# Transposed modulation tiles, two up projections ahead of their norm's root, and first weight blocks split in halves by three engines

## The chip, the cores and the metric

One core of one Trainium2 chip runs the kernel. The metric is the device time of one execution in microseconds. It was 2487.04 us in the median of three runs of the kernel before (2485.96 to 2487.86). Engines are named as in the profile: PE (TensorE), PEld (its weight loads), DVE (VectorE), ACT (ScalarE), POOL (GpSimd), SP (SyncE, which here only issues transfers).

## The reference

512 tokens of 1024 features pass two hybrid layers and a diffusion-style block with neighbourhood attention; everything is float32.

```python
def hybrid_layer(x, ...):                       # twice
    cb, cc, cu, q, k, v, g, ga, gb = split(rmsnorm(x, norm_mix) @ w_in)
    merged = sigmoid(ga) * short_conv_mixer(cb, cc, cu) + sigmoid(gb) * retention_mixer(q, k, v, g)
    x = x + merged @ w_o
    return x + square(relu(rmsnorm(x, norm_mlp) @ w_up)) @ w_down
# once, after rmsnorm(x, norm_final); h and hc are the modulated norms of x and of the context
sh1, sc1, g1, sh2, sc2, g2 = split(silu(c) @ w_mod + b_mod)      # also for c_ctx: csh1, csc1
q, k, v = heads(h @ w_q), heads(h @ w_k), heads(h @ w_v)         # 16 heads, kc and vc from hc
x = x + g1 * (neighbourhood_attention(q, k, v, kc, vc, rpb) @ w_o)
h2 = rms_norm(x, norm2) * (1 + sc2) + sh2
a, g = split(h2 @ ffn_w_up)                                      # 2816 features each
x = x + g2 * ((a * gelu(dwconv3(g))) @ ffn_w_down)
```

## The kernel before, in words

The stream X stays in SBUF, features on the partitions (8 tiles of 128), tokens along the columns (512). Every dense product is made to float32 accuracy from three products of reduced parts: high x high, high x low, low x high (`product`, L526). Weights arrive in blocks of 128 output features (128x1024, 512 KB) in a ring of four slots. SP issues the transfers; ACT copies a block to its high part (L987; the first three in `first_high`, L1054); POOL subtracts to get the low part in four operations of 256 columns (`low`, L464); PE then runs the block's job of 24 products into PSUM bank n % 4, and DVE or ACT evacuates it. Semaphores count: `w_hi_ready`, `w_lo_ready` (blocks), `jobs_done` (jobs), `bank_free` (evacuated), `tiles_ready` (input tiles split).

**Start.** SP issues X and the first four blocks alternately; ACT issues parameters (L976) and positions (L977) and waits for both. It then makes for each pair of X tiles the high parts H_hi (L1027), one block's high part, and squares (L1078). DVE makes H_lo (L1330), the rope angles and the sum of squares. The value job comes first; unlike the others it takes tokens as stationary operand, and a block holds two k tiles of 512 value columns, so one tile is 12 products. After two of the eight blocks PE sums the squares (L548, L550), ACT takes the root (L1020, L1022), DVE the reciprocal (L1367, L1368). DVE evacuates the values in two batches (L1471 to L1309), then q and k, then decays the retention scores (ST, L1309).

**Modulation.** In each of the eight groups of the two layers' feed-forward parts, ACT fetches six tiles of modulation weights (3 MB), DVE multiplies by the condition and adds over the eight k tiles (L1662; in layer 0 also four context tiles, `ctx_acc`). What is left is a sum over the partitions. PE makes it by a product of each 128x128 tile with a two-column tile of ones (L680, L685), into one PSUM bank; at a layer's end DVE adds the bias (L1701) and makes the gains.

**Attention.** For each of eight pairs of heads (t) there are four steps (p). PE turns probabilities (L793, transposes against an identity), computes the next scores (L780), weighs values (L809, L813). The order of all this, and of the dense jobs of the next heads and of the output projection's first products that fill the gaps, is written out by hand. `output(m, first, last)` is output job m's products for k tiles first to last - 1; tile k exists once the k-th pair of heads is done. `turn_values` transposes values (L763).

**Before FF2.** Output jobs 0 to 3 are opened during the attention, job 4 has its weights in a place of its own (`wo_hi`), 5 to 7 follow. DVE adds each to X (L1881) and sums squares (L1321, L1325). PE sums over partitions in two parts (`split_sum`, L839, L841), ACT takes the root (L1022), DVE the reciprocal (L1723), then `adaptive` makes the eight input tiles: scaled (L1726, DVE), high (L1066, ACT), low (L1738, DVE).

**FF2.** 22 pairs of up jobs (gate, value) in three groups, each followed by down jobs. ACT copies the gate (L1283), DVE convolves it (L1901 to L1906), ACT applies gelu (L1286), DVE multiplies by the value job's bank (L1911) and splits. In a round of four jobs ACT's loop (`phase`) alternates one block's high part (`ahead`) with its gates.

## Time and profile before

| | us |
|---|---|
| median of the runs | 2487.04 |
| profiled execution, its own time | 2488.34 |
| its span | 2486.5 |
| PE busy | 2449.0 |
| POOL busy | 1380.8 |
| DVE busy | 1291.5 |
| ACT busy | 819.5 |

The span reaches from the first to the last instruction. PE's busy time includes the overlap of pipelined products, so its pace is read from the distance between the starts of two products rather than from the length of one. A row of the timeline gives start, duration, engine, line, operation, output and inputs, the number of merged instructions, and in brackets the engine's idle time before it and what ended it.

### The profile page before, as it was taken

How to read it: one execution, taken by the hardware profiler on the slowest of the kernel's cores; microseconds unless marked ns; L12 is line 12 of the kernel's file. 1: busy time of each engine (PE TensorE's matmuls, PEld its weight loads, DVE VectorE, ACT ScalarE, POOL GpSimd, SP SyncE). 2: the span in 40 equal slices, each digit the busy share in tenths (PEclk: the TensorE clock that was granted, in tenths of full speed). 3: DMA queues.
4: the chain of work that ended last, by engine and by line, in shares of the span. 5: the costliest groups of instructions: out<-in, count | busy, mean ns of one | idle time of the engine just before them, and what ended most of it. 6: DMA issues, size and time to landing. Idle time of an engine off the chain costs nothing.

```text
span 2486.5 us, 33193 instructions
## 1 busy us (share of the span) xinstructions
PE 2449.0 (98%) x11372; PEld 2004.7 (81%) x11372; DVE 1291.5 (52%) x1828; ACT 819.5 (33%) x1053; POOL 1380.8 (56%) x1676
## 2 busy tenths in 40 slices
PE   7999999999999999999999999999999999899999
PEld 6888888888888888888888888888777776788887
DVE  8984412354645659944123535438866665533323
ACT  4232232231211222322322311114567774432222
POOL 6556655656666655566556566647332334455654
PEclk9999999999999999999999999999999999999999
DMA  5213223243334222133232433443211112232322
GB/s 177 93 60 97 97 93 101 93 146 129 114 136 144 96 96 87 60 98 96 93 101 93 147 133 109 144 152 102 67 52 39 60 47 69 77 100 93 101 93 93
DMA packets 64455, 247.46 MB, mean 100 GB/s; under 512 B 7152, under 2 KB 9584, under 8 KB 63088
## 3 DMA queue, kind: packets, MB, share of 16 engines
q1 hardware_dynamic: 61920, 217.87, 27.0%
q10 hardware_dynamic: 2448, 28.43, 2.9%
q8 instruction: 54, 0.88, 0.1%
q14 instruction: 33, 0.27, 0.0%
HBM read 244.17 MB, written 2.10 MB: 99 GB/s over the span
## 4 chain that ended last, share of the span: by engine, by line
PE 89%; DVE 7%; DVEq 2%; issue 1%; ACT 1%; DMA 0%; ACTq 0%
PE ps L526 84%; PE ps L793 1%; PE ps L780 1%; PE ps L809 1%; PE ps L748 1%; DVE A_lo L1309 1%; DVE A_lo_f L1505 1%; DVEq L1306 0%; DVEq L1503 0%; DVE V_lo L1309 0%; DVE C_hi_f L1501 0%; DVE A_hi L1307 0%; ACT prob L1195 0%; DVE C_hi_f L1500 0%; PE ps L813 0%
## 5 line engine op out<-in xcount | busy, mean ns | idle before, releaser
L464 POOL TENSOR_TENSOR w_lo<-w_raw,w_hi 128x256 fp32r<-128x256 f32 x1612 | 1334.9, 859 | 1005.9 <-ACT w_hi L987 873.6
L526 PE MATMUL ps<-H_hi,w_hi 128*128 128x512 f32 x1952 | 776.2, 398 | 6.6 <-DVE H_lo L1738 6.6
L526 PE MATMUL ps<-H_hi,w_lo 128*128 128x512 f32 x1952 | 762.3, 391 | 0.0
L526 PE MATMUL ps<-H_lo,w_hi 128*128 128x512 f32 x1952 | 762.1, 390 | 0.0
L987 ACT ACTIVATE w_hi<-w_raw 128x1024 fp32r<-128x1024 f32 x400 | 421.3, 1056 | 989.7 <-PE ps L526 955.4
L526 PEld LDWEIGHTS ps<-H_hi,w_hi 128*128 128x128 f32 x1952 | 368.0, 189 | 90.4 <-issue 16.3
L526 PEld LDWEIGHTS ps<-H_lo,w_hi 128*128 128x128 f32 x1952 | 368.2, 189 | 78.6 <-issue 4.8
L526 PEld LDWEIGHTS ps<-H_hi,w_lo 128*128 128x128 f32 x1952 | 367.7, 188 | 77.4
L526 PE MATMUL ps<-A_lo,w_hi 128*128 128x512 f32 x552 | 215.3, 390 | 0.0
L526 PE MATMUL ps<-A_hi,w_hi 128*128 128x512 f32 x496 | 193.0, 389 | 0.0
L526 PE MATMUL ps<-A_hi,w_lo 128*128 128x512 f32 x496 | 192.9, 389 | 0.0
L1342 DVE TENSOR_TENSOR X<-X,ps 128x512 f32<-128x512 f32 x80 | 55.0, 688 | 206.4 <-PE ps L526 206.1
L526 PE MATMUL ps<-C_hi,w_hi 128*128 128x512 f32 x384 | 149.4, 389 | 0.0
L526 PE MATMUL ps<-C_lo,w_hi 128*128 128x512 f32 x384 | 149.4, 389 | 0.0
L526 PE MATMUL ps<-C_hi,w_lo 128*128 128x512 f32 x384 | 149.4, 389 | 0.0
L526 PEld LDWEIGHTS ps<-A_lo,w_hi 128*128 128x128 f32 x552 | 104.1, 189 | 21.1
L1644 DVE TENSOR_TENSOR E<-ps,rstd 128x512 f32<-128x512 f32 x64 | 44.2, 690 | 128.3 <-PE ps L526 127.7
L526 PEld LDWEIGHTS ps<-A_hi,w_hi 128*128 128x128 f32 x496 | 93.1, 188 | 19.5 <-DVE A_lo L1309 0.2
L526 PEld LDWEIGHTS ps<-A_hi,w_lo 128*128 128x128 f32 x496 | 93.1, 188 | 19.4
L526 PE MATMUL ps<-B_hi,w_hi 128*128 128x512 f32 x248 | 98.3, 396 | 0.0
L526 PE MATMUL ps<-B_hi,w_lo 128*128 128x512 f32 x248 | 97.3, 392 | 0.0
L526 PEld LDWEIGHTS ps<-C_hi,w_hi 128*128 128x128 f32 x384 | 72.1, 188 | 15.0
(255 smaller groups left out, 2911.3 us busy)
## 6 DMA issues: line engine op xcount, KB each, us to landing
w_raw<-weights SPq DMA_DIRECT2D x404, 512.0 KB, 3.5
mod_w<-mod_weights ACTq DMA_DIRECT2D x8, 3072.0 KB, 10.9
X<-x SPq DMA_DIRECT2D x4, 512.0 KB, 7.5
out<-X SPq DMA_DIRECT2D x8, 256.0 KB, 2.0
toeplitz<-biases SPq DMA_DIRECT2D x14, 128.0 KB, 2.0
decay_sb<-decay ACTq DMA_DIRECT2D x1, 1024.0 KB, 5.1
ctx_sb<-context ACTq DMA_DIRECT2D x1, 1024.0 KB, 15.4
mask_sb<-key_mask ACTq DMA_DIRECT2D x1, 320.0 KB, 3.0
```

Source lines behind the costliest of these rows:

```text
L464: last = nc.gpsimd.tensor_tensor(lo[:, c:c + LOW_COLS], w_raw[:, q, c:c + LOW_COLS], hi[:, c:c + LOW_COLS].bitcast(F32), ALU.subtract)
L526: mm = nc.tensor.matmul(dst, w[l], xs[r], start=start and a == 0, stop=stop and a == 2)
L748: nc.tensor.matmul(dst, block_sb[:, :], src[:, :], start=True, stop=True).then_inc(sum_ready[kind], 1)
L780: mm = nc.tensor.matmul(ps[:, SCORE_BANKS[head], :], (q_hi, q_lo)[l][rows, T % 2, i * P:(i + 1) * P], (k_hi, k_lo)[r][rows, first:first + ...
L793: mm = nc.tensor.transpose(ps[:, TURN_BANK, c * P:(c + 1) * P], prob[:, head, at_col:at_col + P], ident_sb[:, :])
L809: nc.tensor.matmul(ps[cols[head], OUT_BANK, o0:o0 + 2 * P], v_sb[:, T % 2, tile, cols[head]], pt[:, head, c, :, :].rearrange("p t n -> p ( ...
L987: nc.scalar.activation(w_hi[:, s, :], w_raw[:, s, :], ACT.Copy).then_inc(w_hi_ready, 1)
L1309: V.tensor_tensor(lo, whole, hi.bitcast(F32), ALU.subtract).then_inc(ready, 1)
L1342: V.tensor_tensor(X[:, m, :], X[:, m, :], ps[:, q, :], ALU.add).then_inc(bank_free, 1)
L1505: V.tensor_tensor(Alf[:, m, :], Cf[:, 0, :], Cf[:, 1, :], ALU.add)
L1644: V.tensor_tensor(E[:, q % 2, :], ps[:, q, :], rstd[:, :], ALU.mult).then_inc(bank_free, 1)
```

## The change

**Modulation.** Each modulation tile is transposed on PE against the identity (10 tiles a group in layer 0, 6 in layer 1, into banks 5 to 7), and DVE sums along the columns after each group (`mod_reduced`). The identity is loaded at the start, to a place of its own, not before the attention. DVE also splits the shift SH2 in two reduced parts.

**Start.** The wait for the positions moves to DVE, ahead of the angles. Blocks 0 and 1 are made in halves: high halves by ACT between its H_hi tiles, first low half by DVE, second by POOL. Squares come one pair later; the sum over partitions stands after the third block in layer 0.

**Attention's end.** The output products are distributed otherwise over the gaps of the last two pairs of heads, `turn_values(7, 1)` is moved, job 4 gets bank 5 and is opened in the last step (`output_ahead`), job 5 gets weights of its own (`w5_hi`, `w5_lo`).

**Late root.** ACT and DVE split X times gain (without the root) into C_hi and C_lo as each output tile is added, and ACT makes the squares. The first two FF2 jobs (gate 0, value 0) run on these parts. DVE multiplies the two banks by the root afterwards; what the shift adds to each output feature comes from 32 two-column products (`up_shifts`). The first round of FF2 is taken out of the loops.

```diff
 # PE
-                        if i == 0 and q == 2:
+                        if i == 0 and q == (2 if L else 3):
                             norm_sum(2 * L, True)
-                        pe.wait_ge(w_lo_ready, n0 + i * RING + (q + 1))
+                        halves = L == 0 and i == 0 and q < 2
+                        if halves:
+                            pe.wait_ge(first_low, q + 1)
+                        else:
+                            pe.wait_ge(w_lo_ready, n0 + i * RING + (q + 1))
...
                     pe.wait_ge(mod_summed, L * FF_GROUPS + g + 1)
-                    for s in range(MOD_GROUP):
-                        at_col = (g * MOD_GROUP + s) * 2
-                        mm = nc.tensor.matmul(ps[:, MOD_BANK, at_col:at_col + 2], mod_w[:, s, 0:P],
-                                              ones[:, 0:2], start=True, stop=True)
...
+                    pe.wait_ge(mod_reduced, L * FF_GROUPS + g)
+                    summed = [mod_w[:, s, 0:P] for s in range(MOD_GROUP)]
                     if L == 0:
+                        summed += [ctx_acc[:, s, :] for s in range(MOD_CTX)]
+                    for s, src in enumerate(summed):
+                        mm = nc.tensor.transpose(ps[:, MOD_BANK + s // TOK, s % TOK * P:(s % TOK + 1) * P], src,
+                                                 ident_sb[:, :])
                     mm.then_inc(mod_used, 1)
...
+            def up_shifts(n):
+                pe.wait_ge(shift_split, 1)
+                for q in range(2):
+                    for k in range(DT):
+                        for part, w in enumerate(weight_tiles(n + q, k)):
+                            mm = nc.tensor.matmul(ps[:, SHIFT_BANK, 2 * q:2 * q + 2], w, shift_parts[:, k, :],
+                                                  start=k == 0 and part == 0, stop=k == DT - 1 and part == 1)
+                mm.then_inc(shift_mm, 1)
...
                     if t == TILES - 2 and p == 3:
-                        output(0, 5, 6)
-                        output(1, 0, 1)
+                        turn_values(T, 1)
+                        output(1, 3, 4)
                     if t == TILES - 1 and p == 0:
-                        output(1, 4, 6)
+                        output(2, 0, 2)
                     if t == TILES - 1 and p == 1:
-                        output(2, 3, 5)
-                    if t == TILES - 1 and p >= 2:
-                        output(3, 2 * p - 2, 2 * p)
+                        output(3, 0, 2)
+                    if t == TILES - 1 and p == 2:
+                        output(3, 4, 6)
+                    if t == TILES - 1 and p == 3:
+                        output_ahead(0, 2)
...
+                    if t == TILES - 1 and p == 3:
+                        output_ahead(2, 3)
...
                     if t == TILES - 2 and p == 2:
-                        output(0, 2, 5)
-                        turn_values(T, 1)
+                        output(0, 2, 6)
+                        output(1, 0, 3)
                     if t == TILES - 2 and p == 3:
-                        output(1, 1, 4)
+                        output(1, 4, 6)
                     if t == TILES - 1 and p == 0:
-                        output(2, 0, 3)
+                        output(2, 2, 6)
                     if t == TILES - 1 and p == 1:
-                        output(2, 5, 6)
-                        output(3, 0, 2)
-            for m in range(WO_AHEAD):
-                output(m, 6, 7)
+                        output(3, 2, 4)
+                    if t == TILES - 1 and p == 2:
+                        for m in range(WO_AHEAD):
+                            output(m, 6, 7)
+            output_ahead(3, 5)
             for m in range(WO_AHEAD):
                 output(m, 7, DT)
+            output_ahead(5, DT)
...
-            split_sum(2 * DEPTH + 1, last_squared, 1)
...
                 if g == 0:
                     pe.wait_ge(w_lo_ready, n + 2)
...
+                    up_shifts(n)
+                    split_sum(2 * DEPTH + 1, wo_squared, DT)
+                    pair_job(n, 0, wo_parts, 0, C_hi, C_lo)
+                    pair_job(n, 2, tiles_ready, ATT_TILE + DT, H_hi, H_lo)
 # ACT
-            act.wait_ge(par_loaded, 32)
+            act.wait_ge(par_loaded, 16)
             for j in range(X_PARTS):
...
                     stream_high(m, PAR_NORM1, 0)
-                if j < RING - 1:
+                    if j < 2:
+                        first_half(j, m % X_PART)
+                if j == 2:
                     first_high(j)
...
+            act.dma_start(ident_sb[:, :], ident).then_inc(ident_loaded, 16)
...
+                        act.wait_ge(w_loaded[1], (WO_ROUND + 2) * 16)
+                        act.wait_ge(ctx_mm, 2 * TILES)
+                        nc.scalar.activation(w5_hi[:, :], w_raw[:, 1, :], ACT.Copy).then_inc(w_hi_ready, 1)
+            def wo_parts_high(m):
+                act.wait_ge(bank_free, WO_JOB + m + RING + 1)
+                nc.scalar.activation(E[:, SQUARES[m % 2] if m else SUMSQ, :], X[:, m, :],
+                                     ACT.Square).then_inc(wo_squared, 1)
+                nc.scalar.activation(C_hi[:, m, :], X[:, m, :], ACT.Copy,
+                                     scale=gains[:, 2 * DT + m:2 * DT + m + 1]).then_inc(wo_high, 1)
+            for m in range(DT):
+                wo_parts_high(m)
+                if m < 2:
+                    ahead_at(WO_JOB + 6 + m)
+                if m >= RING:
+                    ahead_at(WO_JOB + RING + m)
             root(2 * DEPTH + 1, E[:, ROOT, :])
-            high_parts(1, SH2)
+            high_parts(1, SH2, WO_JOB + DT + RING)
...
+                if g == 0:
+                    gate(r, 0, 0)
+                    ahead(r, 2)
+                    gate(r, 0, 2)
+                    ahead(r, 3)
+                    tile0, rounds = m0 + 2, rounds - 1
 # DVE
+            def first_low_half(q):
+                dve.wait_ge(first_split, q + 1)
+                V.tensor_tensor(w_lo[:, q, 0:V_WIDE], w_raw[:, q, 0:V_WIDE], w_hi[:, q, 0:V_WIDE].bitcast(F32),
+                                ALU.subtract).then_inc(first_low, 1)
...
+                    dve.wait_ge(mod_used, L * FF_GROUPS + g + 2)
+                    first = (L * FF_GROUPS + g) * MOD_GROUP
+                    reduced = V.tensor_reduce(by_tile(mod, first, MOD_GROUP), mod_turns[:, 0:MOD_GROUP, :], AX_X, ALU.add)
...
+                    reduced.then_inc(mod_reduced, 1)
...
             adaptive(2 * DEPTH + 1, 2 * DT, SH2)
+            fence()
+            job_done(FF2_ROUND, 0)
+            V.tensor_tensor(E[:, 0, :], ps[:, 0, :], E[:, ROOT, :], ALU.mult).then_inc(scaled_up, 1)
+            job_done(FF2_ROUND, 1)
+            V.tensor_tensor(E[:, 1, :], ps[:, 1, :], E[:, ROOT, :], ALU.mult).then_inc(bank_free, 2)
 # SP
+            sp.wait_ge(first_low, 2)
             load_rounds(1, ATT_ROUND)
```

## Rows read from the trace of the kernel before

**Rows 1.** The page: busy time by engine, and POOL's low parts.
```profile
PE 2449.0 (98%) x11372; PEld 2004.7 (81%) x11372; DVE 1291.5 (52%) x1828; ACT 819.5 (33%) x1053; POOL 1380.8 (56%) x1676
...
L464 POOL TENSOR_TENSOR w_lo<-w_raw,w_hi 128x256 fp32r<-128x256 f32 x1612 | 1334.9, 859 | 1005.9 <-ACT w_hi L987 873.6
```
**Rows 2.** Waits of PE: waited for, us in total, times, longest.
```profile
PE ps L526 <- POOL w_lo L464: 13.8, 1, 13.8
PE ps L526 <- DVE H_lo L1738: 6.6, 1, 6.6
PE ps L793 <- ACT prob L1201: 3.6, 2, 3.0
PE ps L763 <- DVE v_sb L1826: 2.7, 2, 2.3
```
**Rows 3.** Waits of DVE between 11 and 118 us, the longest.
```profile
DVE C_hi_f L1476 <- issue: 0.5, 1, 0.5
```
**Rows 4.** Timeline, the start to the first retention product, several engines.
```profile
7.37 1.33 ACT L1027 ACTIVATE H_hi<-X,par 128x512 fp32r<-128x512 f32 x2 [0.89 <-DMA z_pos<-positions]
...
8.61 1.04 ACT L1054 ACTIVATE w_hi<-w_raw 128x1024 fp32r<-128x1024 f32 x1
...
13.81 0.77 PE L526 MATMUL ps<-w_hi,H_hi 128*128 128x512 f32 x1 [13.81 <-POOL w_lo L464]
...
26.58 1.05 PE L548 MATMUL ps<-ones,E 128*128 128x2 f32 x8
...
28.64 0.27 ACT L1020 ACTIVATE token_rstd<-ps,eps 128x8 f32<-128x8 f32 x1 [5.85 <-PE ps L550]
...
30.57 0.20 DVE L1367 RECIPROCAL token_rstd<-token_rstd 128x8 f32<-128x8 f32 x1
...
61.41 0.68 DVE L1471 TENSOR_REDUCE small<-ps 128x2 f32<-128x512 f32 x1
...
118.14 0.73 PE L526 MATMUL ps<-ST,V_hi 128*128 128x512 f32 x2 [0.86 <-DVE ST L1309]
```
**Rows 5.** DMA issues at 1.19: times issued, KB, us to landing.
```profile
w_raw<-weights SPq DMA_DIRECT2D x1, 512.0 KB, 5.9
```
**Rows 6.** Windows: us, busy by engine, granted PE clock, DMA share and GB/s.
```profile
615.00:618.00 3.00, 3.00 (x9) 2.32 (x8) 0.00 (x0) 1.06 (x1) 1.59 (x3) 0.52 0.84 262
...
2072.00:2084.50 12.50, 8.86 (x53) 6.16 (x52) 1.72 (x9) 5.14 (x10) 2.67 (x4) 0.86 0.15 43
```
**Rows 7.** Timeline of PE, the first modulation group of layer 0.
```profile
612.34 1.39 PE L680 MATMUL ps<-ones,mod_w 128*128 128x2 f32 x12
...
614.49 0.77 PE L526 MATMUL ps<-H_hi,w_hi 128*128 128x512 f32 x1
```
**Rows 8.** Timeline of PE, four transposes in the attention and the next product.
```profile
2032.00 0.60 PE L793 MATMUL ps<-ident_sb,prob 128*128 128x128 f32 x4
2032.36 0.48 PE L526 MATMUL ps<-H_hi,w_hi 128*128 128x512 f32 x1
```
**Rows 9.** Timeline of DVE, behind the last modulation group.
```profile
1755.14 3.35 DVE L1745 RECIPROCAL rstd_sq<-rstd_sq 128x512 f32<-128x512 f32 x1 [1.35 <-ACT rstd_sq L1214]
```
**Rows 10.** Timeline, the attention's last scores and turn, and output job 0's evacuation.
```profile
2073.96 0.50 PE L780 MATMUL ps<-k_hi,q_hi 64*128 64x512 f32 x2
...
2077.88 0.66 PE L793 MATMUL ps<-ident_sb,prob 128*128 128x128 f32 x4 [2.96 <-ACT prob L1201]
...
2088.05 1.15 DVE L1881 SCALAR_TENSOR_TENSOR X<-ps,mod,X 128x512 f32<-128x512 f32 x1 [1.52 <-PE ps L526]
```
**Rows 11.** Timeline, the root ahead of FF2, its first product, the first gelu.
```profile
2114.95 0.69 ACT L1022 ACTIVATE E<-ps,eps 128x512 f32<-128x512 f32 x1 [6.11 <-PE ps L841]
...
2121.54 0.77 PE L526 MATMUL ps<-H_hi,w_hi 128*128 128x512 f32 x1 [6.62 <-DVE H_lo L1738]
...
2137.63 1.28 ACT L1286 ACT_TABLE_LOAD   x1 [2.61 <-DVE conv L1906]
```
**Rows 12.** One line's instructions: duration in ns, least, median, longest.
```profile
L793 PE MATMUL ps<-ident_sb,prob x256: 270/272/477, 1793.8 to 2081.2; 128*128 128x128 f32 x128
```

More of the change, by code:

```diff
@@ L462, in low @@
                 pool.wait_ge(w_hi_ready, n + 1)
[L463 removed]
+                for c in range(V_WIDE if first else 0, BLK, LOW_COLS):
                     last = nc.gpsimd.tensor_tensor(lo[:, c:c + LOW_COLS], w_raw[:, q, c:c + LOW_COLS],
@@ L471, in low_rounds @@
                         low(i * RING + q, q)
+            for n in range(RING):
+                low(n, n, first=n < 2)
             for L in range(DEPTH):
                 core = L * LAYER_JOBS + JOB_G + EARLY_G + RING - 1
-                low_rounds(L * LAYER_JOBS // RING, core // RING)
+                low_rounds(L * LAYER_JOBS // RING + (L == 0), core // RING)
                 for n in range(core // RING * RING, core):
@@ L515, in _ @@
             low(WO_JOB + WO_AHEAD, 0, wo_hi[:, :], wo_lo[:, :])
-            for q in range(1, RING):
+            low(WO_JOB + WO_AHEAD + 1, 1, w5_hi[:, :], w5_lo[:, :])
+            for q in range(2, RING):
                 low(WO_JOB + RING + q, q)
```

211 lines of the change are left out of this document (145 added, 66 removed).

## The prediction

> **What bounds the kernel now.** I read the page first: TensorE is busy for 98% of the span [rows 1], so the whole margin is its idle time, its slow time and work it need not do. Next its list of waits [rows 2]: the first product waits 13.8 us for the low parts of the first weight block, 6.6 us are lost ahead of the second feed-forward part (FF2), and some 6 us in the attention's last rounds, on probabilities and values. Then I asked where another engine is as full. VectorE in the first layer is: between 11 and 118 us it waits for nothing longer than 0.5 us [rows 3]. The reader should see in the start's timeline [rows 4] that VectorE takes the second half of the value evacuation at 61.41, just when TensorE has finished it, and that from there its own queue decides the first retention product at 118.14.
>
> A 512-column product starts 0.227 us after the last (both levels of the clock can be read off the start-to-start times: 0.227 at the 2.4 GHz level, 0.427 at 1.2). All sums below are against the profiled execution (2488.34 us, span 2486.5); the median of the runs is 2487.04, 1.3 less.
>
> **Part 1, the start.** Three edits act together: parameters are waited for without the positions, the first two blocks are split in halves, and VectorE makes two of the low halves. ScalarE could start at 6.47 (the table load ends there) instead of 7.37, where it waited for the positions [rows 4]. Block 0 has landed at 1.19 + 5.9 = 7.1 [rows 5]. H_hi 0.65, half a copy 0.55 (half of 1.04, plus overhead): 7.7; H_lo on VectorE to 7.95, its half block 0.7 to 1.07: the first product comes at 8.8 instead of 13.81, so 5.0 us earlier. The later half blocks are in time: GpSimd's two operations follow at 8.9, and one value tile of 12 products lasts 2.7 us.
>
> But this does not get through. The norm sum now stands one block (5.45 us) later: 8.8 + 4.2 (12 products, the first 3 us at half speed) + 5 x 2.72 = 26.6, the very time of before, 26.58. ScalarE's root then ends at 29.5 as before, and VectorE, which started its reciprocals at 30.57 [rows 4], can gain at most about 1.0. Up to there it carries 1.4 to 2.1 us more (two half blocks), starts 0.9 earlier, and is less disturbed since GpSimd has 12 operations instead of 16. After it VectorE's queue is full to 118 [rows 3], so the first retention product comes 0 to 1.5 us earlier. TensorE arrives 5 us early and waits there about 5 us in one piece. Around a wait of 2.96 us the mean granted clock is 0.86 in the trace [rows 6], since half-speed products follow it; that costs 0 to 1.6 us here. I take 0 for the whole start (bounds: 1 lost, 1.5 gained). The identity load's issue on ScalarE (0.4) is covered by the wait for the norm sum; SP's added wait for the two half blocks ends near 12, with three blocks in hand.
>
> **Part 2, the modulation.** Removed: two records of two columns for each of 48 stream tiles and 16 context tiles. A first-layer group has 20 of them: 612.34 to 614.49 [rows 7], 2.15 us, 0.105 to 0.108 each. After two of the four groups the clock fell: granted 0.52 in the three microseconds behind the first [rows 6], that is the 1.2 GHz level, which costs 1.65 us each time (8 products at 0.427). A second-layer group has 12: 1.25 us. Added: 10 or 6 transposes. Four in the attention take 2032.00 to 2032.36, 0.09 each [rows 8]: 0.9 and 0.54. First layer: 4 x 1.25 + 2 x 1.65 = 8.3. Second layer: 3 x 0.7 = 2.1. The last group yields 0: behind it the attention's first H_lo tiles set the pace with no slack, and VectorE's queue there grows by a reduction and the split of the shift (1.5, of columns and small operations) where it had waited 1.35 for a root [rows 9]. VectorE's reductions (0.96 for 768 columns, 0.69 for 512, by the 0.69 of a 512-column one [rows 4]) and its wait for the transposes stand ahead of the next up projection's evacuation, whose product ends 5.45 us later: hidden. **Sum 10.4** (bounds 7.1, if both drops of the clock stay, and 11.1).
>
> The row is nearest for the transpose: same data type, same identity, same engine. What speaks against it is told with the rivals.
>
> **Part 3, the attention's last two heads.** Nothing is removed; output products are placed in other gaps, and a fifth and sixth output job get weights of their own. From scores to the turn that needs them takes 3.92 (2073.96 to 2077.88, with nothing in between [rows 10]); a copy of the turned tile is ready 1.3 after its turn. I walked the new order with these: turn 27 still waits for VectorE's least values (0.7) and for its first copy (0.6); 12 products behind scores 29 and 31 leave 0.3 each of the wait; the sixth job's high part (1.04) on ScalarE's queue stands ahead of the copy of turn 30 and costs 1.15; small ones 0.8. Together 3.8, where before it was 11.4, read off the starts between 2039.6 and 2084.6: 6.6 of the listed waits [rows 2], 2.9 of half speed behind the two longest, 1.9 in gaps too short to be listed. Output job 0 ends at 2083.65 instead of 2087.8 [rows 10], and since five eighths of job 4 are done ahead, the last output product ends at 2104.05 instead of 2111.66: **7.6** (bounds 5.6 and 9).
>
> **Part 4, the late root.** Times from 2083.65. VectorE needs some 3.1 us per tile (residual 1.15, low part 0.75 to 1.19, sum 0.7 to 1.07), so tile 7 is updated at 21.6; the last output product ends at 20.4. GpSimd has the two up blocks at 20.2 (0.86 x 4 per block [rows 1], behind ScalarE). Added: 32 two-column products, 0.105 each by the modulation's rate, 3.4 us: 23.9. The norm sum: 25.7. Then the two late-root jobs, 10.9 us, hide root, reciprocal and the first H_lo, which before took 2114.95 to 2121.54 [rows 11]: H_lo 0 comes at 32.3, TensorE needs it at 36.6. The next two jobs end at 47.5. All this at full clock; the small products are 3.4 us of what made the clock fall after 2.15 us in Part 2, and this may cost up to 2.7 (1.1 in the small products and norm sum, 1.6 behind).
>
> What is late next is ScalarE and GpSimd. VectorE scales the two late banks only after the eight H_lo (42.7), so: gated tile 44.1, convolution 46.6, gelu with its table load 48.7 (1.28 [rows 11] and 0.72), block 13 of the stream split at 49.7, low by 53; then the second gate the same way, block 14 high at 56.5, low at 59.9. TensorE could take it at 58.4. With the clock lost it comes at 60 and waits for nothing. Either way the third job of the next round starts at 60.0 to 61.0, 2144.2; before it started at 2121.54 + 1.6 + 144 x 0.2266 = 2155.8. That is 11.6 for Parts 3 and 4, so **4.0** for this one (bounds 1.5 and 6.4).
>
> **Sum:** 0 + 10.4 + 7.6 + 4.0 = 22.0. From 2488.34: 2466.3; from the median 2487.04: **2465.0**.
>
> **The rivals.**
> (a) The start's saving gets through. For: 5.0 us at the first product are sure. Against: VectorE's queue without a gap [rows 3]. If its evacuations run clear of GpSimd's, or the order has slack that I missed: 2465.0 - 4.9 = 2460.1. Chance 0.10.
> (b) The turned tiles cost as much as the multiplied ones. A transpose's record lasts 0.272 [rows 12]; if groups of ten run at that rather than at 0.09, 64 x 0.272 = 17.4, against 4 x 2.15 + 4 x 1.25 + 3.3 = 16.9 before: nothing is gained and the forecast loses 10.4 + 0.5: 2475.9. Against: the next product followed four of them after 0.36. Chance 0.08. The Trainium skill (TensorE: Matmul & The Clock Gate, Part 4: PE-mode transpose) gives about 275 ns for one in a kernel and says that the fast clock does not engage for them; by that rule this rival is the result. The row's duration agrees, its start-to-start does not.
> (c) The gap ahead of FF2 only changes its owner: half speed through the 32 small products, and both late-gate blocks waited for. Part 4 gives 0: 2469.0. For: all three engines are within 1 us of each other there. Chance 0.13.
> (d) Slower. The gates of FF2 keep ScalarE behind: the first pair of gates starts about 2 us late, and if each of the eleven rounds made TensorE wait over 22.0 / 11 = 2.0 us for a weight block, the gain is gone; at 2.6 it is 2493.6. Against: before, the same order of copies and gates ran with no such wait, and a pair on VectorE takes about 7 us of 10.9. Chance 0.02.
> (e) The change does not do what it says: the waits return in other places of the same size, 2487. Chance 0.03.
>
> **Chances and range.** Forecast 0.64, (a) 0.10, (b) 0.08, (c) 0.13, (d) 0.02, (e) 0.03. A measurement of this kernel tells about 0.2% (5 us) from no change. Faster: 0.64 + 0.10 + 0.08 + 0.13 = 0.95; within 0.2%: 0.03; slower: 0.02. All lower bounds together give -1 + 7.1 + 5.6 + 1.5 = 13.2, 2473.8; the upper ones 1.5 + 11.1 + 9 + 6.4 = 28.0, 2459. The range takes these and (a) and (c), 2458 to 2475, and leaves out (b), (d), (e): 0.13.
>
> **What would show it.** First product near 8.8; norm sum near 26.6; one TensorE wait of about 5 us for VectorE's ST in the first layer (none: (a) is right). From the first transpose of a modulation group to the next product 0.9 (first layer), with no half-speed stretch behind (2.7: (b)). Last output product some 7.6 earlier against the end of the second layer. The 32 small products in 3.4 us, the norm sum right behind; no wait for H_lo; a wait for w_lo of 0 to 2 us in FF2's second round. The prediction is wrong if VectorE waits in the first layer before 118, if turned groups last over 1.5 us, or if FF2 waits for weights in later rounds.

## The result, and the profile after

The changed kernel takes 2469.89 us (median of 4 runs, 2465.40 to 2471.63); the kernel before took 2487.45 beside it (median of 4, 2485.96 to 2489.76). The ratio is 0.9922, 95% interval 0.991 to 0.9935: 17.6 us faster, where 22.0 were forecast. The profiled execution took 2471.63, its span is 2469.8, 16.7 less than before; the parts below are read against that.

Two lines of the page of the changed kernel, the answer to [rows 1]:

```profile
PE 2444.0 (99%) x11340; PEld 1999.8 (81%) x11340; DVE 1305.6 (53%) x1847; ACT 819.6 (33%) x1064; POOL 1375.6 (56%) x1672
...
L486 POOL TENSOR_TENSOR w_lo<-w_raw,w_hi 128x256 fp32r<-128x256 f32 x1608 | 1330.2, 858 | 988.8 <-ACT w_hi L1054 855.5
```

Its longest waits of TensorE, which answer to [rows 2] (waited for: us in total, times, longest):

```profile
PE ps L551 <- DVE w_lo L1537: 9.0, 1, 9.0
PE ps L551 <- DVE ST L1420: 5.9, 2, 5.0
PE ps L826 <- ACT pt L1292: 2.2, 3, 1.3
PE ps L781 <- ACT sq_q L1268: 1.8, 1, 1.8
PE ps L704 <- DVE ctx_sum L1755: 0.8, 1, 0.8
```

The big waits of before (13.8 for the first block, 6.6 for H_lo, 3.6 and 2.7 for probabilities and turned values) are gone or down. One is new: 5.0 us for ST, in one piece, in the first layer, as forecast.

The start, from the timeline of the changed kernel (start, duration, engine, line, what, idle time before and its releaser), the answer to [rows 4]:

```profile
9.03 0.76 PE L551 MATMUL ps<-w_hi,H_hi 128*128 128x512 f32 x1 [9.03 <-DVE w_lo L1537]
...
28.29 0.95 PE L575 MATMUL ps<-ones,E 128*128 128x2 f32 x8
...
31.12 0.20 DVE L1478 RECIPROCAL token_rstd<-token_rstd 128x8 f32<-128x8 f32 x1 [1.40 <-ACT rstd L1089]
...
61.60 0.68 DVE L1591 TENSOR_REDUCE small<-ps 128x2 f32<-128x512 f32 x1
...
119.10 1.22 PE L551 MATMUL ps<-ST,V_hi 128*128 128x512 f32 x2 [5.03 <-DVE ST L1420]
```

The first product comes 4.8 us earlier, yet the first retention product comes 1.0 **later** than before (118.14). The windows of the changed kernel (window, length, busy by engine, granted PE clock, DMA share, GB/s), the answer to [rows 6], show what follows on that wait:

```profile
118.00:121.00 3.00, 1.90 (x5) 1.52 (x6) 2.78 (x6) 0.00 (x0) 0.00 (x0) 0.50 0.00 0
121.00:124.00 3.00, 3.00 (x11) 2.81 (x10) 2.04 (x7) 0.63 (x1) 0.00 (x0) 0.50 0.00 0
615.00:618.00 3.00, 3.00 (x20) 2.61 (x19) 2.04 (x3) 0.74 (x1) 0.04 (x1) 1.00 0.58 168
...
2100.00:2103.00 3.00, 3.00 (x19) 3.00 (x18) 2.64 (x5) 2.98 (x4) 3.00 (x3) 0.60 0.41 154
2103.00:2106.00 3.00, 3.00 (x7) 1.76 (x8) 0.16 (x1) 0.05 (x1) 2.33 (x4) 0.50 0.54 175
```

Behind the wait TensorE runs at the 1.2 GHz level for 5 us, which costs another 2.1: the third gate job starts at 145.68, before at 142.67. **The start loses 3.0 us** in this pair of traces. The 1.0 at the first retention product can be followed on VectorE: its reciprocals start 0.55 later than before, the time up to the second value batch is 0.36 shorter, the batch itself 0.8 longer (15.75 against 14.95, with the same operations, several of which last longer), and the stretch from the first query tile to ST the same (41.0 in both). The third window is the first modulation group: clock 1.00, where it was 0.52. The last two are the small products of the late root: 0.60 and 0.50.

TensorE's timeline of the changed kernel at that group and at the late root, the answer to [rows 7] and [rows 11]:

```profile
615.36 0.82 PE L718 MATMUL ps<-ident_sb,mod_w 128*128 128x128 f32 x6
616.01 0.60 PE L718 MATMUL ps<-ident_sb,ctx_acc 128*128 128x128 f32 x4
616.37 0.48 PE L551 MATMUL ps<-H_hi,w_hi 128*128 128x512 f32 x1
...
2097.99 0.39 PE L551 MATMUL ps<-B_hi,w_lo 128*128 128x512 f32 x1
2098.57 0.27 PE L887 MATMUL ps<-shift_parts,w_hi 128*128 128x2 f32 x1 [0.19 <-POOL w_lo L486]
...
2103.61 2.06 PE L906 MATMUL ps<-E,ones 128*128 128x512 f32 x2
```

Ten tiles are turned in 1.01 us (616.37 - 615.36). Followed from landmark to landmark, before against after: start +3.0; the first layer's four groups -7.9 (2.8, 2.7, 1.2 and 1.2), the second layer's first three -2.1, of which 0.9 is lost again at 1676 in a wait for the context's squares (ctx_sum above), the last group -0.5: **modulation -9.5**; **attention -6.9** (the last output product starts at 2097.99, before at 2111.43, less the 6.5 that it was ahead already); **late root -3.3**. Together -16.7. (The expectations below have 7.2 and 3.0 for these two, from 2111.66, where in the kernel before the norm sum starts.)

### The profile page after: what moved, and what is told of

The parts are those of the page before. It is cut to its first block, busy times and chain, and to the rows that moved or that the text cites. A ratio compares the mean times of both kernels' runs of the same rounds, so it can differ in the third digit from the quotient of the medians.

```text
span 2469.8 us, 33125 instructions
## 1 busy us (share of the span) xinstructions
PE 2444.0 (99%) x11340; PEld 1999.8 (81%) x11340; DVE 1305.6 (53%) x1847; ACT 819.6 (33%) x1064; POOL 1375.6 (56%) x1672
## 4 chain that ended last, share of the span: by engine, by line
PE 88%; DVE 6%; DVEq 2%; ACT 1%; issue 1%; DMA 1%; POOL 1%; ACTq 0%; POOLq 0%
PE ps L551 83%; PE ps L813 1%; PE ps L826 1%; PE ps L842 1%; DMA ctx_sb<-context 1%; PE ps L781 1%; DVE A_lo L1420 1%; DVE A_lo_f L1625 1%; POOL w_lo L486 1%; DVEq L1623 0%; DVE V_lo L1420 0%; DVE C_hi_f L1621 0%; DVE A_hi L1418 0%; ACT prob L1278 0%; DVE C_hi_f L1620 0%
## 5 line engine op out<-in xcount | busy, mean ns | idle before, releaser
L551 PE MATMUL ps<-H_hi,w_hi 128*128 128x512 f32 x1936 | 767.9, 397 | 0.6 <-issue 0.3
L551 PE MATMUL ps<-H_hi,w_lo 128*128 128x512 f32 x1936 | 754.4, 390 | 0.0
L551 PE MATMUL ps<-H_lo,w_hi 128*128 128x512 f32 x1936 | 754.1, 389 | 0.0
L551 PE MATMUL ps<-C_hi,w_hi 128*128 128x512 f32 x400 | 156.6, 392 | 0.0
L551 PE MATMUL ps<-C_hi,w_lo 128*128 128x512 f32 x400 | 155.7, 389 | 0.0
L551 PE MATMUL ps<-C_lo,w_hi 128*128 128x512 f32 x400 | 155.7, 389 | 0.0
```

Of the source, the lines that this page charges most:

```text
L551: mm = nc.tensor.matmul(dst, w[l], xs[r], start=start and a == 0, stop=stop and a == 2)
```

## The experiments

Each kernel is the changed kernel with one edit, unless said otherwise. The ratio is to the kernel before on the same chip; the three groups ran on different chips, so between groups ratios are compared, and 0.001 is 2.5 us.

**The base.** The changed kernel again.

> The changed kernel again, beside the others on one chip: 2469.9 us by the runs so far (before 2487.4, ratio 0.993). It is the base for the three runs beside it.

Measured: 2469.59 us (2468.70 to 2471.06, 5 runs), ratio 0.9925 (0.9911 to 0.9938).

Single traces have to be compared with care, since three places vary between executions of the same code. The half speed at the launch lasts 4.3 to 6.1 us in the ten traces with the changed start, and the two of the changed kernel have 6.0 and 6.1; in four later runs (the modulation undone, every tile turned twice, the late root undone, the output order undone), whose code is the same up to there, it lasts 4.3 to 5.1, the first retention product comes at 118.2 to 118.6 and the third gate job at 144.3 to 145.0, so that by them the start loses 1.6 to 2.3 us instead of 3.0. The wait for the context's squares is anything from 0 to 1.4. And in six traces the clock falls between the 18th and the 25th of the 32 small products, and from the last output product to the end it takes 371.8 us; in four it falls only behind them, and that takes 370.2.

**The start undone.**

```
-            act.wait_ge(par_loaded, 16)
+            act.wait_ge(par_loaded, 32)
...
-                    if j < 2:
-                        first_half(j, m % X_PART)
...
+                if j < RING - 1:
                     first_high(j)
...
-                        if i == 0 and q == (2 if L else 3):
+                        if i == 0 and q == 2:
                             norm_sum(2 * L, True)
```

> Only the start is as it was before; the rest is the changed kernel. Theory (VectorE's queue bounds the first 120 us, and the start's edits give it more and start its reciprocals later): 3.0 us faster than the changed kernel, 2466.9; first product near 13.8, norm sum near 26.6, VectorE's reciprocals at 30.6 instead of 31.1, TensorE's wait for ST in the first layer 0.9 instead of 5.0, and no stretch at half speed behind it. Rival 1 (the 3.0 us come from another part, such as the identity's load or GpSimd's order): same as the changed kernel, 2469.9, and the third output job of the retention still starts at 145.7. Rival 2 (the start is a gain that the landmarks hide): slower, up to 2474.

Measured: 2467.96 us (2467.55 to 2468.30, 5 runs), ratio 0.992 (0.9906 to 0.9933). 1.6 faster than the base by the medians, 3.5 by the two profiled spans (2465.8 and 2469.3). All five runs lie below all five of the base. The base's spans reach from 2466.9 to 2469.3, and the profiled one is its longest. But of the changed kernel's four runs in the result one took 2465.40 (its mean granted clock was 0.999, that of the other three 0.997; it has no trace), so the sign holds for this pair of medians and not for every execution. From TensorE's timeline:

```profile
118.36 0.73 PE L550 MATMUL ps<-ST,V_hi 128*128 128x512 f32 x2 [0.86 <-DVE ST L1413]
...
2099.75 1.63 PE L905 MATMUL ps<-E,ones 128*128 128x512 f32 x2
```

The wait for ST is 0.86 again, and no slow stretch stands behind it: the third gate job starts at 142.89, 2.65 ahead of the base. Of that 1.05 goes in a longer wait for the context's squares, which leaves 1.6 at the attention, the size that the medians show. The other 1.9 of the 3.5 arise behind it, 1.6 of them because the small products take 3.6 us at full clock (the norm sum follows at 2099.75) where the base's take 4.7. Whether that follows from the start's edits or is chance is not shown. Rival 1 and rival 2 fall.

**VectorE relieved.** If the queue of VectorE is the bound, 5.5 us less in it should come back whole.

```
-                        if i == 0 and q == (2 if L else 3):
+                            if L == 0 and i == 0 and q == 2 and kk == 1:
+                                norm_sum(0, True)
...
+            pool.wait_ge(sines_ready, 3)
+            for a in range(2):
+                turned = nc.gpsimd.tensor_tensor(turns[:, a, :], rope[:, a, :], rstd[:, :], ALU.mult)
+            turned.then_inc(turns_ready, 1)
...
+                    nc.scalar.activation(rstd_sq[:, :], rstd[:, :], ACT.Square)
```

> The changed kernel with VectorE relieved in the first layer: norm sum one value tile earlier, the two products of sines and root on GpSimd, the root's square and the sign of the sines on ScalarE. Theory (VectorE's queue is the bound, and a long wait of TensorE costs half speed behind it): VectorE's queue is 5.5 us shorter (1.4 + 2.4 + 0.9 + 0.9); TensorE's wait for ST falls from 5.0 to at most 0.7 and the stretch at half speed behind it goes, 2.1: 5.5 to 7 us faster than the changed kernel, 2463 to 2464.4. Rival 1 (GpSimd's two products delay weight low parts and disturb VectorE by the shared port): the wait moves to w_lo, gain 0 to 2: 2468 to 2470. Rival 2 (ST is late for another reason than the queue's length): the wait for ST stays over 4 and the gain is under 1.

Measured: 2470.46 us (2469.04 to 2471.09, 5 runs), ratio 0.9929 (0.9915 to 0.9942). No gain, as rival 2 had it: TensorE still waits 4.34 us for ST. The relief arrived: VectorE now reaches the second value batch early enough to wait for TensorE. From there its timeline reads (the last row is TensorE's):

```profile
57.57 0.69 DVE L1600 TENSOR_REDUCE small<-ps 128x2 f32<-128x512 f32 x1 [1.08 <-PE ps L556]
...
73.26 0.69 DVE L1631 TENSOR_TENSOR C_hi_f<-ps,turns 128x512 f32<-128x512 f32 x1 [0.19 <-issue]
...
94.61 0.69 DVE L1631 TENSOR_TENSOR C_hi_f<-ps,turns 128x512 f32<-128x512 f32 x1
...
100.06 0.69 DVE L1631 TENSOR_TENSOR C_hi_f<-ps,turns 128x512 f32<-128x512 f32 x1
...
117.05 0.69 DVE L1430 TENSOR_TENSOR ST<-st_tmp,ST 128x512 fp32r<-128x512 f32 x1
117.80 1.22 PE L556 MATMUL ps<-ST,V_hi 128*128 128x512 f32 x2 [4.34 <-DVE ST L1430]
```

It starts the eight tiles of queries and keys (L1631 is the first operation of each) at 73.26, where the changed kernel starts them at 77.35, and ends the first ST only 1.3 earlier. Of the lead of 4.1 the tiles eat 2.8: they start 5.04 us apart once and then 5.43 to 5.51, which is TensorE's time for one job (24 x 0.2266 = 5.44), though nothing in VectorE's rows waits for TensorE: its idle time between 73.2 and 117.8 adds up to 3.1 us, against 2.7 for the same operations in the changed kernel, and no gap is over 0.45. In the changed kernel the same steps are 4.56, 4.18, 4.72, 5.11, 5.45, 5.49 and 5.45. **My theory (a full queue) is wrong here**; what holds the tiles at TensorE's pace was the question of the next group.

**The same relief with the start as before** (the norm sum where it was).

> The same relief (but the norm sum where it was before) with the start as before. Theory: TensorE, which starts at 13.8, is the bound here, and VectorE's waits cost it 0.9: 0.9 faster than the run with the start alone undone, 2466.0, and so 2 to 3 us slower than the relief with the start's edits. Rival (the start's edits are worth nothing in any case): equal to the relief with the start's edits within 0.5 us.

Measured: 2468.10 us (2466.26 to 2470.13, 5 runs), ratio 0.9922 (0.9908 to 0.9935): nothing gained over the start alone undone (2467.96), and 2.4 faster than the relief with the start's edits, so that neither the theory nor the rival fits. VectorE waits 4.47 us for TensorE at 61.66 and ends the first ST at 118.3, as with the start alone undone. So this relief is worth nothing with either start.

**GpSimd quiet.** Of the low parts of blocks 13 to 20 only the last quarter is computed, so GpSimd's bursts of four operations become one. This kernel leaves work out and serves only to ask for the cause.

```
-            for n in range(RING):
-                low(n, n, first=n < 2)
+            for n in range(5 * RING + 1):
+                low(n, n % RING, first=n < 2, start=BLK - LOW_COLS if n >= 13 else None)
```

> The changed kernel, but of the low parts of the weight blocks 13 to 20 (the ones that GpSimd splits between 69 and 112 us) only the last quarter is computed; the other three quarters stay those of earlier blocks, so GpSimd has one operation for a block instead of four. Theory (VectorE's tiles of queries and keys last 5.44 us because GpSimd's burst, released by TensorE once a product of 5.44 us, always falls on VectorE's SBUF operations; alone they last 4.2): VectorE's eight tiles start 4.2 to 4.4 us apart instead of 4.2 to 5.5, the first ST is ready at 113 to 115 instead of 119.0, TensorE's wait for it falls from 5.0 to 0 to 1 and the stretch at half speed behind goes: 5 to 7 us faster than the changed kernel, 2463 to 2465. Rival (the tiles' pace is VectorE's own): pace, wait and time as in the changed kernel, 2469.6.

Measured: 2461.22 us (2459.04 to 2462.26, 4 runs), ratio 0.9891 (0.9874 to 0.9907): 8.4 faster than the base, more than the 5 to 7 expected. Two tiles side by side, first the sixth in the timeline of the changed kernel (VectorE and GpSimd), then the third in this one, where GpSimd's one operation is over before the three that read only SBUF:

```profile
101.37 0.69 DVE L1619 TENSOR_TENSOR C_hi_f<-ps,turns 128x512 f32<-128x512 f32 x1
...
102.83 3.46 POOL L486 TENSOR_TENSOR w_lo<-w_raw,w_hi 128x256 fp32r<-128x256 f32 x4 [2.04 <-ACT w_hi L1054]
103.56 1.25 DVE L1625 TENSOR_TENSOR A_lo_f<-C_hi_f 128x512 f32<-128x512 f32 x1
104.88 0.81 DVE L1418 CAST A_hi<-A_lo_f 128x512 fp32r<-128x512 f32 x1
105.77 1.07 DVE L1420 TENSOR_TENSOR A_lo<-A_lo_f,A_hi 128x512 fp32r<-128x512 f32 x1
106.86 0.69 DVE L1619 TENSOR_TENSOR C_hi_f<-ps,turns 128x512 f32<-128x512 f32 x1
```

```profile
84.25 0.69 DVE L1622 TENSOR_TENSOR C_hi_f<-ps,turns 128x512 f32<-128x512 f32 x1
84.96 0.74 POOL L486 TENSOR_TENSOR w_lo<-w_raw,w_hi 128x256 fp32r<-128x256 f32 x1 [4.32 <-ACT w_hi L1057]
...
86.44 0.69 DVE L1628 TENSOR_TENSOR A_lo_f<-C_hi_f 128x512 f32<-128x512 f32 x1
87.20 0.43 DVE L1421 CAST A_hi<-A_lo_f 128x512 fp32r<-128x512 f32 x1
87.71 0.69 DVE L1423 TENSOR_TENSOR A_lo<-A_lo_f,A_hi 128x512 fp32r<-128x512 f32 x1
88.43 0.69 DVE L1622 TENSOR_TENSOR C_hi_f<-ps,turns 128x512 f32<-128x512 f32 x1
...
112.81 0.73 PE L554 MATMUL ps<-ST,V_hi 128*128 128x512 f32 x2 [0.24 <-DVE ST L1423]
```

With a burst alongside, the three operations that read only SBUF last 1.25, 0.81 and 1.07; without one 0.69, 0.43 and 0.69. Those fed from PSUM last 0.69 in both. The tile goes from 5.49 to 4.18 (all seven steps of this run are 4.18 to 4.67), TensorE's wait for ST from 5.03 to 0.24, its first retention product from 119.10 to 112.81 (6.3), and no half speed follows (2.1). That is 8.4; a wait of 0.8 for the context's squares falls away too, and the two traces differ by 9.3. About 1.0 of the 6.3 is the launch, whose half speed lasted 4.4 us in this execution and 6.1 in the other; from the first query tile to ST the stretch is 4.8 shorter (36.2 against 41.0). The rival falls. The chain, read from the releasers in the rows, is: TensorE ends a job, ScalarE copies a block, GpSimd's burst starts, and VectorE's SBUF operations stretch until the tile is as long as the job, 5.44. Once they are in step they stay so in these traces, and a head start is then not turned into an earlier ST. That the step is held by this, and not met by chance, is argued: six of the seven steps are 5.43 to 5.51 in the relief run, and again in two runs below, but where the burst falls in the tile was not varied by itself. The Trainium skill (SBUF — State Buffer, Who interferes with whom) has the rule: a VectorE instruction with two SBUF inputs contends with a GpSimd instruction that reads SBUF, casts can too, and one with at most one SBUF input outside the fast modes does not. These rows agree with it.

**The values' scaling on ScalarE.** A way to use this without leaving work out: ScalarE is idle 4.4 of every 5.44 us there.

```
+                                for h in range(2):
+                                    done = nc.scalar.activation(Cf[:, t, h * RV:(h + 1) * RV],
+                                                                ps[:, i * TOK + t, h * RV:(h + 1) * RV], ACT.Identity,
+                                                                bias=stat[:, 2 * t + h:2 * t + h + 1],
+                                                                scale=token_rstd[:, 2 * t:2 * t + 1])
...
+                            V.tensor_scalar(stat[:, 2 * t:2 * t + 2], small[:, 2 * t:2 * t + 2], -1.0 / RV,
+                                            token_rstd[:, 2 * t:2 * t + 1], ALU.mult, ALU.mult).then_inc(means_ready, 1)
...
+                            dve.wait_ge(v_scaled, i * TOK + t + 1)
+                            high = V.tensor_copy(V_hi[:, t, cols], Cf[:, t, :])
```

In the first layer this takes the place of VectorE's own scaling, and it also changes VectorE's order: sums and means of all four tokens first, then the copies and the low parts. The run tests both together.

> The changed kernel with the scaling of the first layer's values (subtract the mean, times the token's root) on ScalarE; VectorE keeps sums, means and splits. It takes 1.0 + waits off each of 8 value tiles on VectorE. Theory: VectorE starts the tiles of queries and keys at 67 to 70 us instead of 77.35; even at the locked pace of 5.44 it is then near TensorE, first ST at 114 to 115, the wait for ST 0 to 1.5 instead of 5.0, no half speed behind: 4 to 7 us faster than the changed kernel, 2463 to 2466. Rival 1 (the lead is eaten by GpSimd's bursts as in the relief run): first ST at 117 or later, gain under 1.5, 2468 to 2470. Rival 2 (ScalarE's copies of weight blocks come late behind the scaling): waits for w_lo appear between 44 and 70 us, 2470 or slower.

Measured: 2463.33 us (2461.74 to 2464.79, 4 runs), ratio 0.9903 (0.9887 to 0.992): 6.3 faster than the base by the medians, 5.5 by the ratios, and 24.8 faster than the kernel before, **the fastest version here that leaves nothing out**. Its timeline:

```profile
46.95 3.73 ACT L1186 ACTIVATE C_hi_f<-ps,stat,token_rstd 128x256 f32<-128x256 f32 x8
...
68.81 0.69 DVE L1657 TENSOR_TENSOR C_hi_f<-ps,turns 128x512 f32<-128x512 f32 x1 [0.16 <-issue]
...
113.62 0.73 PE L554 MATMUL ps<-ST,V_hi 128*128 128x512 f32 x2 [0.86 <-DVE ST L1437]
```

The tiles start 8.5 us earlier and then fall into the same step (94.68, 100.12, 105.56), but this time one job of TensorE sooner than in the relief run, and the wait is 0.86. Rivals 1 and 2 fall. Here too the small products run at full clock; that is 1.6 of the 8.6 by which this trace is ahead of the base's, and not a part of the reason above.

**The same with the start as before.**

> The values' scaling on ScalarE as in the run before, but with the start as it was before the change. Theory (with this start TensorE reaches the first ST at 117.5 us itself, so that a shorter queue on VectorE is worth at most the 0.9 that TensorE waited there): 2467 to 2468, 4 us slower than the same kernel with the start's edits (2463.3). Rival (the values' edit is a gain by itself, whatever the start): 2463 to 2464.

Measured: 2466.98 us (2466.56 to 2470.46, 5 runs), ratio 0.9919 (0.9905 to 0.9933), as the theory had it. By the ratios the start's edits are worth 4.0 us here (0.9919 against 0.9903; the intervals overlap, the runs of the two kernels do not), and cost 1.6 without this relief: their sign hangs on what VectorE has to do between them and the first ST. VectorE starts the query tiles at 71.73, 4.9 ahead of the run with the start alone undone, and ends the first ST 0.25 ahead of it: six of its seven steps are 5.43 to 5.45.

**The modulation undone.**

```
-                        mm = nc.tensor.transpose(ps[:, MOD_BANK + s // TOK, s % TOK * P:(s % TOK + 1) * P], src,
-                                                 ident_sb[:, :])
+                        mm = nc.tensor.matmul(ps[:, MOD_BANK, at_col:at_col + 2], mod_w[:, s, 0:P],
+                                              ones[:, 0:2], start=True, stop=True)
```

> Only the modulation is as it was before (products by ones, identity loaded late, no reductions); the rest is the changed kernel. Theory: 9.5 us slower than the changed kernel, 2479: a first-layer group takes 2.15 us again, and the stretches at half speed behind two of the four come back. Rival (a turned tile costs as much as a multiplied one): no difference, 2469.6.

Measured: 2484.22 us (2482.26 to 2487.51, 10 runs), ratio 0.9984 (0.9974 to 0.9994): 14.6 slower than the base (14.7 by the ratios), 5 more than the landmarks gave. Neither expectation fits. The first layer's groups behave as expected (2.15 us each, half speed behind the first and the fourth), 7.9 us. The surprise stands in the second layer, in TensorE's timeline of this run:

```profile
993.80 1.22 PE L551 MATMUL ps<-ST,V_hi 128*128 128x512 f32 x2 [4.33 <-DVE ST L1417]
...
1764.08 0.39 PE L551 MATMUL ps<-HC_hi,w_hi 128*128 128x256 f32 x1 [2.01 <-DMA ident_sb<-identity]
```

In the base TensorE waits 0.86 for ST in the second layer. Here the eight tiles start 5.06 us apart once and then 5.44 to 5.51, as in the relief run, while in the base they run 4.2 to 5.2; that costs 4.8 with the half speed behind it. The late identity costs 2.0 behind the last group. So part of the 14.6 is that this kernel falls into the slow step in a layer whose code is the same. Why it does was not settled: how TensorE's job times stood to VectorE's there was not varied by itself. The traced execution is the slowest of the ten, 3.3 over their median, and the ten spread over 5.3 us, so the others need not all have this step.

**Every tile turned twice.**

```
+                    for again in range(2):
-                    for s, src in enumerate(summed):
+                        for s, src in enumerate(summed):
```

> The changed kernel with every modulation tile turned twice (the second time over the first): 64 more transposes. Theory (0.10 us each): 5.5 to 6.5 us slower, 2476 (2479 if two groups of 2.0 us bring the half speed back behind them, as the products of 2.15 us did). Rival (a transpose costs its record's 0.27 us): 17 us slower, 2487.

Measured: 2476.70 us (2476.26 to 2477.12, 4 runs), ratio 0.9956 (0.9939 to 0.9973): 7.1 slower (7.7 by the ratios), 0.11 to 0.12 for each of the 64. TensorE's timeline of a first-layer group:

```profile
614.37 0.82 PE L719 MATMUL ps<-ident_sb,mod_w 128*128 128x128 f32 x6
...
615.46 0.82 PE L719 MATMUL ps<-ident_sb,mod_w 128*128 128x128 f32 x6
...
616.47 0.47 PE L551 MATMUL ps<-H_hi,w_hi 128*128 128x512 f32 x1
```

20 transposes take 2.10 us, 0.105 each, at full clock behind all four groups. The rival (0.27) falls. The Trainium skill (TensorE: Matmul & The Clock Gate, Part 4: PE-mode transpose) gives about 275 ns for one (of bf16, in one kernel) and says that the fast clock does not engage for them. Here one float32 record lasts 0.272, which agrees, but they start 0.105 apart, and the granted clock around a group of ten is 1.00.

**The late root undone.**

```
-                    up_shifts(n)
-                    split_sum(2 * DEPTH + 1, wo_squared, DT)
-                    pair_job(n, 0, wo_parts, 0, C_hi, C_lo)
-                    pair_job(n, 2, tiles_ready, ATT_TILE + DT, H_hi, H_lo)
+                    for k in range(DT):
+                        pe.wait_ge(tiles_ready, ATT_TILE + DT + k + 1)
```

> Only the late root is undone (the first two up projections wait for the scaled tiles again, no small products); the rest is the changed kernel. Theory by the landmarks of the two traces: 3.0 us slower than the changed kernel, 2472.6. Rival 1 (the small products and the half speed in them eat the gain): no difference, 2469.6. Rival 2 (the forecast's full term): 4.0 slower or more, 2473.6 and above.

Measured: 2472.18 us (2471.44 to 2473.87, 4 runs), ratio 0.9936 (0.9921 to 0.9951): 2.6 slower by the medians, 2.7 by the ratios. The wait of 6.6 for H_lo is back:

```profile
PE ps L551 <- DVE H_lo L1848: 6.6, 1, 6.6
```

From the last output product to the end its trace takes 374.2 us, the base's 371.8. The theory holds.

**The small products left out** (the shift of the first two up projections is zero).

```
-                    up_shifts(n)
```

> The changed kernel without the 32 small products: the shift of the first two up projections is left out (zero). Theory (they stand on the path: norm sum, root, reciprocal and scaled tiles all come behind them): norm sum 3.5 to 4.7 us earlier, no stretch at half speed, and 3.5 to 6 us faster than the changed kernel, 2464 to 2466. Rival (ScalarE's and GpSimd's chain of gates and weight blocks sets the next jobs in any case): a wait for w_lo or for the gates takes the place, under 1 us faster, 2469.

Measured: 2468.24 us (2467.19 to 2469.21, 4 runs), ratio 0.9918 (0.9903 to 0.9933): 1.4 faster by the medians, 1.7 by the ratios. Neither expectation fits. TensorE's timeline tells why:

```profile
2100.96 2.04 PE L906 MATMUL ps<-E,ones 128*128 128x512 f32 x2 [3.30 <-DVE E L2016]
```

Without them TensorE waits 3.30 us in their place for VectorE's sum of squares. The 32 products, 3.4 us by the forecast and 3.6 at full clock, mostly fill a wait that is there anyway. From the last output product to the end it is 369.5 us without them, 370.2 with them where the clock does not fall in them, and 371.8 where it does: most of what they cost is the half speed that begins in them. (The two norm sums behind run at it in this trace and in the base's.)

**The output order undone.**

```
-                    if t == TILES - 1 and p == 3:
-                        output_ahead(0, 2)
...
-            output_ahead(3, 5)
             for m in range(WO_AHEAD):
                 output(m, 7, DT)
-            output_ahead(5, DT)
+            output_ahead(0, DT)
```

> Only TensorE's order of output products in the last two heads is as before (the fifth job after the attention, the turned values late); weights, banks and the late root stay as in the changed kernel. Theory: 7.2 us slower than the changed kernel, 2476.8; the waits of 2.2 for v_sb and of 3.0 for prob return with half speed behind them. Rival (the gain came from the fifth and sixth jobs' own weight buffers, which stay here): 0 to 3 us slower, 2470 to 2472.

Measured: 2475.12 us (2474.52 to 2475.58, 4 runs), ratio 0.9947 (0.9931 to 0.9962): 5.5 slower than the base, between theory and rival. From its waits of TensorE:

```profile
PE ps L826 <- ACT prob L1279: 4.0, 3, 3.0
PE ps L796 <- DVE v_sb L1952: 2.7, 2, 2.3
```

Both long waits of before are back, so the order is what removed them. From the attention's first wait for sq_k to the last output product it takes 336.9 us, in the base 330.8 and before 337.7: the order gives 6.1 of 6.9, and the rival falls as the main cause. What is missing in the total stands behind: from there to the end this trace is 2.1 shorter than the base's (369.7), and 0.9 of it are the small products, where the clock falls only at the 30th.

## Why the prediction was right, and where it was not

The total was right (2465.0 within 2458 to 2475; measured 2469.9), and in three of its four parts the reasons were right in the main. Every part fell short of its forecast, by 3.0, 0.9, 0.7 and 0.7, which is the 5.3 between 22.0 and the 16.7 of the traces. Undone one at a time the parts are worth -1.6, 14.6, 5.5 and 2.6; that is 21.1, more than the 17.6 of the whole, because the modulation undone brings the slow step and the late identity with it, in its trace at least.

**Part 1, the start: wrong in size and in reason.** The step read: the norm sum at 26.6, "the very time of before", then VectorE's full queue, so 0, bounds -1 and +1.5. The norm sum came at 28.29: after the first product TensorE ran at half speed for 6.1 us instead of the 3 that I had taken over, 1.4 more, and VectorE waited 1.40 for the root, a wait that the prediction named as a sign against it. The first ST was then 1.0 later instead of 0 to 1.5 earlier. Behind the wait of 5.03 (forecast: "about 5") the half speed cost 2.1, above my bound of 1.6. Together -3.0 in this pair of traces, -1.6 by the medians; other executions had 4.3 us of half speed at the launch and lost 1.6 behind the wait, so both misses are partly this execution's. The step that failed is that VectorE would start its reciprocals up to 1.0 earlier: they started 0.55 later, and the second value batch took 0.8 more. The reason, "VectorE's queue is full", was read off [rows 3] as if the queue's length were given. The prediction knew that GpSimd disturbs VectorE, and put no price on it. The same tile lasts 4.18 or 5.49, by where GpSimd's burst falls, and 5.5 us taken out of the queue brought nothing. A queue without gaps whose period is TensorE's 5.44 need not be full; it can be in step. This did not make the loss of 1.0, for the eight tiles took 41.0 us before and after; it is why less work on VectorE does not bring it back.

**Part 2, the modulation: right.** 10.4 forecast, 9.5 in the traces. The first layer gave 7.9 of 8.3 and the second 2.1 of 2.1, at 0.10 for each turned tile where [rows 8] had 0.09, and the last group 0.5 where nothing was forecast; what was missed is a wait of 0.8 for the context's squares in the last group, which costs 0.9. Undone alone it is worth 14.6, for the second layer's step and the late identity come on top. Rival (b) is out.

**Part 3, the attention's tail: right.** 7.6 forecast, 6.9 in the traces, 5.5 by the run that undoes the order alone (6.1 within the attention). Its "6.6 of the listed waits" is 3.6 for prob, 2.3 of the 2.7 for v_sb, and 0.7 for pt, which [rows 2] does not show.

**Part 4, the late root: right in size, one step wrong.** 4.0 forecast, 3.3 in the traces and 2.6 undone alone. The step that failed is the 3.4 us of small products, put on the path: tile 7's squares come later than I reckoned, and the products stand in that wait. They took 5.0 because the clock fell inside them, for which the prediction had held up to 2.7 ready. No wait for H_lo over 0.2 came, as forecast, and the longest wait for a weight block behind the start is 0.5.

Rival (a), the start's saving gets through, is true of one kernel here, the one with the values' scaling on ScalarE. Rival (c) happened in its first half, the clock in the small products, but not in its price: 3.3 of the gap are gone. Rivals (d) and (e) left no trace.

## What to carry to other kernels

When an engine shows no waits, look at the durations of one operation over time before calling its queue full: VectorE's SBUF operations stretch beside GpSimd, and if GpSimd is released by TensorE's job, VectorE's tile can fall in step with that job, so that a lead need not come through (a lead of 4.1 us gave 1.3, one of 4.9 with the start as before 0.25, one of 8.5 gave 5.5), and a shorter burst on GpSimd gave more here (8.4) than less work on VectorE (0 and 6.3). An edit that lets TensorE begin earlier can be a loss while another engine decides the next meeting point: here 4.8 us turned into one wait of 5.0, and the clock fell behind it. And before the difference of two traces is put down to an edit, look at what differs between traces of the same code: the clock at the launch and in the small products alone makes over 2 us here.

## What the runs showed of the hardware

Several speeds of one and the same VectorE stretch: from the first reduction of the second value batch to the start of the first ST's last operation it took 56.0, 56.1, 56.1 and 56.0 us (kernel before, both layers; start undone; relief with the start as before), 56.7 in the first layer of the changed kernel, 59.5 and 59.5 (relief; second layer with the modulation undone), and 51.5 with GpSimd's short bursts.

The granted clock: in the changed kernel's trace a wait of 5.03 us was followed by 5 us at the 1.2 GHz level (2.1 lost); in other traces the same wait cost 1.6 to 2.1, one of 4.34 (relief) 1.8, one of 4.33 (second layer with the modulation undone) 1.3, and one of 0.86 nothing. At the launch the half speed lasted 4.3 to 6.1 us from the first product where that stood near 9, and 3.1 to 4.3 where it stood near 14. Twenty two-column products in 2.15 us brought it back behind two of four groups, twenty transposes in 2.10 us behind none, and of the 32 two-column products the 19th was the first slow one in the changed kernel's trace and the 30th in that with the output order undone, and in four traces (start undone, relief with the start as before, values' scaling with either start) none was.
